# Layer 0 spreads the second MLP modulation chunk over half rounds one by one, layer 1 in its general order

## What is computed

```
def modulation(cond, w_mod, b_mod):
    m = jax.nn.silu(cond) @ w_mod + b_mod
    return jnp.split(m[:, None, :], N_MOD, axis=-1)          # six chunks of 1024

def conv_ffn(h, w_up, conv_w, conv_b, w_down):
    z = h @ w_up                                             # 1024 -> 5632
    zp = jnp.pad(z, ((0, 0), (1, 1), (0, 0)))
    z = zp[:, :-2] * conv_w[0] + zp[:, 1:-1] * conv_w[1] + zp[:, 2:] * conv_w[2] + conv_b
    a, g = jnp.split(z, 2, axis=-1)
    return (jax.nn.silu(a) * g) @ w_down

def trunk_layer(x, cond, ctx_k, ctx_v, p):
    sh1, sc1, gt1, sh2, sc2, gt2 = modulation(cond, p['w_mod'], p['b_mod'])
    ...
    h2 = rms_norm(x, p['norm2_g']) * (1.0 + sc2) + sh2
    x = x + gt2 * conv_ffn(h2, p['w_up'], p['conv_w'], p['conv_b'], p['w_down'])
```

## Time and profile before

| | us |
|---|---|
| median of 3 runs | 1437.02 (1436.52 to 1437.05) |
| profiled execution, its own time | 1439.71 |
| its span, first to last instruction | 1437.9 |
| PE busy | 1405.4 (98%) |
| DVE busy | 907.0 (63%) |
| ACT busy | 534.4 (37%) |
| POOL busy | 398.6 (28%) |

### The profile page before, as it was taken

The page is one execution under the profiler, slowest core; times in us unless marked ns, Lnnn a source line. Parts: engine busy times, 40 slices in busy tenths (PEclk is TensorE's granted clock), DMA queues, the critical chain, the costliest instruction groups (busy, mean ns, idle before and its releaser), DMA issues.

```text
span 1437.9 us, 24974 instructions
## 1 busy us (share of the span) xinstructions
PE 1405.4 (98%) x9867; PEld 1347.5 (94%) x9867; DVE 907.0 (63%) x1429; ACT 534.4 (37%) x798; POOL 398.6 (28%) x273
## 2 busy tenths in 40 slices
PE   6999999999999999999999999999999999999998
PEld 3888889999999999999999877999999999999998
DVE  3548879897966478785775887369844323444333
ACT  5427863533231123332242687244232112332332
POOL 0165002053430033434214800213433101323321
PEclk9999999999999999999999999999999999999999
DMA  9752014253535334344413200224323312222321
GB/s 317 226 183 96 2 31 133 90 152 110 163 122 164 94 115 143 124 120 150 125 56 89 62 2 2 59 89 132 103 74 88 90 57 74 73 73 73 101 61 74
DMA packets 198158, 147.03 MB, mean 102 GB/s; under 512 B 4401, under 2 KB 187449, under 8 KB 197049
## 3 DMA queue, kind: packets, MB, share of 16 engines
q1 hardware_dynamic: 196592, 144.27, 32.8%
q10 hardware_dynamic: 1480, 1.57, 0.3%
HBM read 142.94 MB, written 2.88 MB: 101 GB/s over the span
## 4 chain that ended last, share of the span: by engine, by line
PE 83%; DVE 9%; ACT 2%; issue 2%; SPq 1%; DMA 1%; DVEq 0%; ACTq 0%
PE pair L1506 65%; PE pair L1522 7%; PE pair L1916 3%; PE pair L1961 3%; PE pair L1930 2%; DVE mod_acc L1073 2%; DVE conv L1423 1%; DVE in_lo L1139 1%; DVE w_lo L1050 1%; DVE norm_t L1129 1%; SPq L427 1%; DMA w_first<-in_w_mod_dram 1%; DVE small L1352 1%; PE pair L1759 1%; PE pair L1662 0%
## 5 line engine op out<-in xcount | busy, mean ns | idle before, releaser
L1506 PE MATMUL pair<-in_hi,w_hi 128*128 128x384 f32 x1728 | 395.7, 310 | 2.8 <-DVE w_lo L1050 2.8
L1506 PE MATMUL pair<-in_lo,w_hi 128*128 128x384 f32 x1728 | 394.6, 309 | 0.0
L1506 PE MATMUL pair<-in_hi,w_lo 128*128 128x384 f32 x1728 | 393.0, 308 | 0.0
L1423 DVE SCALAR_TENSOR_TENSOR conv<-pair,vec,conv 128x127 f32<-128x127 f32 x352 | 168.6, 542 | 192.8 <-ACT conv L956 192.4
L1506 PEld LDWEIGHTS pair<-in_hi,w_hi 128*128 128x128 f32 x1728 | 264.8, 188 | 8.3 <-DVE w_lo L1050 3.7
L1506 PEld LDWEIGHTS pair<-in_lo,w_hi 128*128 128x128 f32 x1728 | 265.3, 189 | 0.0
L1506 PEld LDWEIGHTS pair<-in_hi,w_lo 128*128 128x128 f32 x1728 | 264.0, 188 | 0.0
L653 POOL TENSOR_TENSOR silu_a<-silu_a,conv 128x640 f32<-128x640 f32 x44 | 108.6, 2469 | 538.7 <-DVE conv L1423 538.7
L956 ACT ACTIVATE conv<-pair,vec 128x640 f32<-128x640 f32 x88 | 77.8, 886 | 409.7 <-PE pair L1506 407.4
L1050 DVE TENSOR_TENSOR w_lo<-w_raw,w_hi 128x1024 fp32r<-128x1024 f32 (+1 forms) x148 | 195.6, 1322 | 38.3 <-ACT w_hi L675 38.0
L675 ACT ACTIVATE w_hi<-w_raw 128x1024 fp32r<-128x1024 f32 (+1 forms) x82 | 97.0, 1183 | 289.7 <-PE pair L1506 272.9
(11 more groups left out here) (210 smaller groups left out, 1773.1 us busy)
## 6 DMA issues: line engine op xcount, KB each, us to landing
w_raw<-in_w_up_dram SPq DMA_DIRECT2D x88, 512.0 KB, 3.8
mod_raw<-in_w_mod_dram SPq DMA_DIRECT2D x64, 512.0 KB, 4.2
w_raw<-in_w_down_dram SPq DMA_DIRECT2D x32, 704.0 KB, 4.6
w_raw<-in_w_in_dram SPq DMA_DIRECT2D x20, 512.0 KB, 4.1
w_first<-in_w_mod_dram SPq DMA_DIRECT2D x16, 512.0 KB, 9.3
w_raw<-in_w_out_dram SPq DMA_DIRECT2D x16, 512.0 KB, 4.0
mod_raw<-in_w_mod_dram SPq DMA_DIRECT2D x4, 1024.0 KB, 5.0
mod_acc<-in_w_mod_dram SPq DMA_DIRECT2D x4, 1024.0 KB, 5.0
```

Source lines behind the costliest of these rows:

```text
L1423: ins = dve.scalar_tensor_tensor(out=conv[:, s, d0:d1], in0=up_result(g, j, s)[:, d0 + sh:d1 + sh], scalar=v(L, V_TAP[t], s * NF + g * FG ...
L1506: ins = pe.matmul(dst[:, a:e], w[:, s, k, :], rhs[:, kk, a:e], start=first and r == 0, stop=last and r == 2)
```

## The change

Only the placing of chunk A's units on VectorE in group 0 changes. The list `((0,), (), (1,), (2, 3))`, which put unit 0 into round 0, unit 1 behind the first half and units 2 and 3 behind the second half of round 1, is gone. In layer 0 each half round from round 1 on gets one unit behind its lo: round 1 gets units 1 and 2, round 2 units 3 and 4, round 3 units 5 and 6, and round 4 unit 7, followed at once by `mod_part_sums(A)`, which stood ahead of round 4. In layer 1 the list is gone too, and the general rule holds: unit 2j+s in round j, half s. PE's, ACT's, POOL's and SP's orders are unchanged.

```
--- before.py
+++ after.py
@@ -1429,17 +1429,27 @@
                                     lo(nxt + s, s, nk)
                             else:
                                 lo(2 * j + (base + 2 + s), s, nk)
-                            if g == 0 and isinstance(j, int) and j in (0, 1) and chunk is not None:
-                                for k in ((0,), (), (1,), (2, 3))[2 * j + s]:
-                                    mod_unit_at(chunk, k, k % 2, k // 2, k == 0)
+                            if L == 0 and g == 0 and j0 == 0:
+                                if not isinstance(j, int):
+                                    mod_unit_at(chunk, 2 * j + (s - 1), 1 - s, j - (1 - s), False)
+                                elif j == 0 and s == 0:
+                                    mod_unit_at(chunk, 0, 0, 0, True)
+                                elif 0 < 2 * j + s - 1 < NK:
+                                    k = 2 * j + s - 1
+                                    mod_unit_at(chunk, k, k % 2, k // 2, False)
+                                if isinstance(j, int) and 2 * j + s == NK:
+                                    mod_part_sums(chunk)
                             else:
                                 mod_unit_at(chunk, 2 * j + (s - 2 * j0), s, j - j0, isinstance(j, int) and j == j0 and s == 0)
                     up_iter(0, base + 2, NK, A)
                     up_iter(1, base + 4, NK, A)
                     with dve.Fori(2, 4) as j:
                         up_iter(j, None, NK, A)
-                    mod_part_sums(A)
-                    up_iter(4, base + 10, NK)
+                    if L == 0 and g == 0:
+                        up_iter(4, base + 10, NK, A)
+                    else:
+                        mod_part_sums(A)
+                        up_iter(4, base + 10, NK)
                     mod_finish(A)
                     up_iter(5, base + 12, NK, B, 5)
                     with dve.Fori(6, 9) as j:
```

## The result

| | before | changed |
|---|---|---|
| median, us | 1437.03 (22 runs, 1436.21 to 1438.48) | 1439.30 (22 runs, 1437.57 to 1442.51) |
| ratio, 95% interval | | 1.0016 (1.0010 to 1.0022) |
| profiled execution, its span | 1437.9 | 1436.4 |
| PE busy in it | 1405.4 | 1404.0 |
| DVE busy in it | 907.0 | 906.6 |

The changed kernel is about 2.3 us slower (1.4 to 3.2 by the interval), and its times spread over 4.9 us where those of before spread over 2.3. The two profiled spans can't be set against each other: the one of before has a stretch of lowered clock in the kernel's opening, 0.92 from 30 to 60 us, the changed one has 1.00 there. So stretches are compared, from one of PE's small products of a reduction to the next; these are fixed points of the program.

A forecast was written before the change was run, and what follows sets the result against it. PE, 98% busy, was taken as the bound, so only its standing still costs time. Layer 0's +1.16 and layer 1's +0.25 sum to +1.4 on the median 1437.02, giving 1438.4 us, range 1436.7 to 1439.8.

The forecast's parts named there:

- layer 1: Layer 1's up-projection opening: one wait of 1.2 us becomes one of 1.6 two tiles earlier, +0.25.
- the loop's entry: Layer 0, PE at linear(10): the loop beginning behind the wait is no longer prepared in advance, +0.20, bounds 0 and 0.5.
- Layer 0: Layer 0's up-projection opening: a wait of some 2.2 us replaces one of 1.2; with the loop's entry, +1.16 in all.
- The wait for w_lo: PE at linear(6) in layer 0's opening: its 1.17 us idle before lo(6) goes away, -1.43.
- the wait for the reduction: PE before mod_reduce(A) in layer 0, near 338.5 us: a new wait of some 2.2 us for mod_part.
- the order of turns: Layer 1, unit 1 beside round 0's gate: POOL's product goes between DVE's two instructions, so linear(4) starts about 1.6 us late.
- rival (a): Layer 1: units meet POOL less than walked through, up to -1.43 there; total 1437.4 down to 1436.7; chance 0.14.
- The sign of being wrong: Layer 1's linear(6) still waiting would mean that the order of turns between DVE and POOL is wrong; no size given.
- rival (d): PE after the 2.2 us stop: granted clock drops, 0.08 of 30 us is 2.4, total 1440.8; chance 0.03.
- (b): Layer 0's reduction costs nothing, as DVE ends it before PE gets there: total 1435.8; chance 0.04.
- (c): DVE's round 4: unit 7 or the reduction collides with round 3's gate, 1.8 on PE's wait, total 1440.2; chance 0.06.
- (e): Linear(6) still waits, as lo(6) has only 2.5 us of room over unit 2: +1.43 on top, 1439.8; chance 0.05.

The follow-up runs named there:

- Layer 0's half alone: The changed kernel with only layer 0's half of the change, layer 1 as in the kernel before: 1440.87 us, +3.5 against before, ratio 1.0024.
- the -2.9: The kernel before with units 1 and 2 behind lo(4) and unit 3 behind lo(5) in both layers: 1434.42 us against 1437.34, ratio 0.9980.

## Why the prediction was right, and where it wasn't

- **The total.** Forecast 1438.4, range 1436.7 to 1439.8, measured 1439.3, and no change by the bound of 0.2%. It is in the range, but 0.2 outside the forecast's own band of 0.7, and in part by luck: two terms that the sum took too high, layer 1 and the loop's entry (1.5 together), stood against two that it left out, the clock and the input projection (2.4 together).
- **Layer 0.** Forecast +1.16. The wait for w_lo went (-1.43), the wait for the reduction came, 2.1 us long, and the new position of linear(10) is +0.98. The +0.20 for the loop's entry behind a wait was not there. From chunk 4's reduction to chunk 6's it is +1.12 where the clock held. The end of each step from lo(9) on came out within 0.04 us of the walk, those before it within 0.15. This half of the mechanism is shown: with the product moved the stop was gone, and -1.40 of the -1.43 stayed.
- **Layer 1.** Forecast +0.25, measured -1.1. The step that failed is the order of turns: "DVE's first to 981.99; POOL's product (1.58 alone) to 983.5; DVE's second to 984.6". DVE's second instruction went ahead of POOL's product, unit 1 ended at 982.73, and linear(4) was 0.27 late and not 1.6. The text named it a near tie in rival (a) and priced it at up to -1.43, with a chance of 0.14. The course that it walked through was sized right, since in the execution where POOL did get its turn the stretch was +0.22; but the chance of the other was far too small. The sign of being wrong that was given for the order of turns, a wait at linear(6), did not appear although the order was wrong; the start of linear(4) showed it.
- **The clock, rival (d).** As a rival for the total, over the bound for slower, it got 0.03 and did not come true. Its mechanism happened in three of four profiles, at 1.54 us instead of the 2.4 taken from the opening, and the sum had no term for it: some 1.2 on average. The argument against it, that the clock held at 1.00 across a stop of 1.17 us, said nothing of one of 2.1, and the 2.4 came from the opening of an execution in which PE stood still for 3.5 us.
- **Not foreseen at all:** the other tie, in layer 1's input projection, +1.2, over four hundred microseconds behind the last instruction that the change moved in layer 0. The forecast said that a total outside the range would mean that something outside the two openings had moved. Something had, with the total inside it.
- **The sum of what was found:** +1.1 (layer 0) - 1.1 (layer 1) + 1.2 (input projection) + 1.54 in most executions, about 3/4 of them by four profiles (1.2 on average), is +2.4; measured +2.3, +2.2 and +1.9. Layer 0's half alone, without the -1.1, would be +3.5 by the same terms, and measured +3.5. The share of executions with a lowered clock is from four profiles only and stays rough.
- Rivals (b), (c) and (e) did not occur: PE waited 2.1 for the reduction, unit 7 ran in 2.47 beside no gate, and linear(6) waited in neither layer.

## What to carry to other kernels

Before work is spread more evenly over an engine's slots, look at what waits for the last piece: here the spread took away a stop of 1.2 us and put the last unit and its reduction onto the matmul engine's path, a stop of 2.1 which in most executions also cost granted clock. Walk the new order through the measured durations, with the turns of engines that exclude each other, and choose an order in which nothing that the matmul engine waits for hangs on which of two such instructions is first; that gave the -2.9. Where a step does start within 0.2 us of its rival, work out both courses and give each a real chance. And where stretches of a trace are compared between fixed points of the program, an effect far from the change shows itself, which medians alone might have booked to the wrong layer.

## What the runs showed of the hardware

- VectorE instructions with two SBUF inputs and GpSimd instructions take turns, each holding the other off for its whole length; a GpSimd instruction's duration in the trace includes its waiting (1.58, 2.54 and 3.73 us for the same product). The Trainium skill, "SBUF — State Buffer", section "Who interferes with whom", states the exclusion and the traces agree. Who is next between two VectorE instructions that follow each other, when GpSimd asked 0.16 us after the first began, came out both ways in one program: 3.78 and 2.54 us in one execution, 2.48 and 3.74 in the next.
- A stop of 2.1 us on TensorE, after over 60 us without one of more than 0.3, was followed by the lower clock level in three executions of four (0.83 granted over the 10 us around it, 1.54 us lost), and by none of two where throwaway products filled all but 0.3 us of it. The stop of 1.17 us before was not: 1.00 was granted from 312 to 322 us. The opening has the same picture, where TensorE waits for w_first: stops of 3.3 and 3.5 us went with a granted clock of 0.91 and 0.92 from 30 to 60 us, and of six executions with a stop of 1.9 to 2.0 us three had 0.95 to 0.97 and three 1.00.
- One VectorE instruction began 0.46 us after what it waited for in one family of programs and 0.11 after in the other, in all of five and nine executions. In the slower of the two traces shown, VectorE's semaphore instruction had ended 0.4 us ahead of it; what fills that time is open.
